# First gate projection of the second block moved into the row gather of the first

## The reference, cut to what matters

```python
h = h + peer(rmsnorm(h, g_ffn[l]), ...)          # gather of chosen rows, dots, weighted sums
h = rmsnorm(h, g_final)
...
proj = x @ w_in_a[a]                             # second block, x is that h
u  = gelu(proj[..., :SG_WIDTH])
gv = gelu(proj[..., SG_WIDTH:2 * SG_WIDTH])
qm = proj[..., 2 * SG_WIDTH:]                    # queries of the memory attention
```

## Time and profile before

| what | us |
|---|---|
| median of three runs | 2060.9 |
| profiled execution, whole | 2064.71 |
| its span, first to last instruction | 2062.8 |
| PE busy in the span | 1768.5 |
| DVE busy | 776.9 |
| gather: first and last issue of L588 | 262.9 to 919.4 |

### The profile page before, as it was taken

How to read it: one execution, slowest core, us unless ns; L and a number is a source line. 1 busy time by engine, 2 the same in 40 slices (tenths; PEclk the granted TensorE clock), 3 DMA queues, 4 the chain that set the end, 5 groups by cost and what they waited for, 6 DMA issues and landing times. The chain is left out here.

```text
span 2062.8 us, 23546 instructions
## 1 busy us (share of the span) xinstructions
PE 1768.5 (86%) x9356; PEld 918.0 (44%) x9356; DVE 776.9 (38%) x1897; ACT 424.3 (21%) x1000; POOL 299.9 (15%) x284
## 2 busy tenths in 40 slices
PE   9999997876655665568999999988899999999887
PEld 7779873552321111124564444333377644433332
DVE  3945178776667777754230000000224300000002
ACT  2481122221221122223111101000223200000001
POOL 0000033543444444430000000000000000000000
PEclk9999998898887667889999999999999999999999
DMA  7237389999999999997789999999964999999997
GB/s 267 93 125 302 143 341 404 397 421 421 420 421 421 421 421 421 421 421 304 315 356 426 426 428 426 428 426 423 420 242 199 378 428 426 427 426 427 426 424 310
DMA packets 81710, 761.82 MB, mean 369 GB/s; under 512 B 9060, under 2 KB 10053, under 8 KB 18102
## 3 DMA queue, kind: packets, MB, share of 16 engines
q1 hardware_dynamic: 43926, 489.35, 56.9%
q0 software_dynamic: 37664, 270.84, 31.9%
HBM read 759.11 MB, written 1.05 MB: 369 GB/s over the span
## 5 line engine op out<-in xcount | busy, mean ns | idle before, releaser
L2683 PE MATMUL bank<-arena 128*64 128x512 f32 x3072 | 680.3, 597 | 42.2 <-DMA arena<-in_w_up 16.8
L1085 PE MATMUL bank<-arena 64*64 64x512 f32 x2032 | 320.4, 784 | 224.4 <-ACT arena L795 224.4
L2683 PEld LDWEIGHTS bank<-arena 128*64 128x64 f32 x3072 | 231.0, 137 | 477.5 <-issue 448.2
L588 POOL DMA_INDIRECT arena<-in_peer_uv,arena x256 | 288.5, 1127 | 614.2 <-PE bank L1085 301.0
L1458 DVE CUSTOM_DVE_ANT_0 arena<-arena 128x1024 f32<-128x1024 f32 x256 | 313.6, 1225 | 156.6 <-DMA arena<-in_peer_uv,arena 153.2
L2811 DVE TENSOR_TENSOR arena<-arena,bank 128x512 f32<-128x512 f32 x32 | 22.0, 687 | 705.7 <-PE bank L2683 705.7
L1085 PEld LDWEIGHTS bank<-arena 64*64 64x64 f32 x2032 | 92.6, 175 | 432.5 <-ACT arena L795 257.0
L844 PE MATMUL bank<-arena 128*128 128x272 f32 (+2 forms) x768 | 144.8, 349 | 0.2 <-ACT arena L614 0.2
L844 PEld LDWEIGHTS bank<-arena 128*128 128x128 f32 x768 | 126.2, 191 | 19.4 <-issue 2.5
L790 ACT ACTIVATE arena<-arena 128x4 f32<-128x4 f32 (+1 forms) x69 | 14.1, 205 | 465.0 <-DVE arena L1458 465.0
L1541 POOL DMA_DIRECT2D arena<-in_w_router x2 | 1.1, 574 | 566.0 <-POOLq L2555 531.3
(11 more groups left out here) (466 smaller groups left out, 1538.0 us busy)
## 6 DMA issues: line engine op xcount, KB each, us to landing
arena<-in_w_gate SPq DMA_DIRECT2D x64, 2048.0 KB, 32.3
arena<-in_w_up SPq DMA_DIRECT2D x56, 2048.0 KB, 32.4
arena<-in_w_down SPq DMA_DIRECT2D x56, 2048.0 KB, 33.2
arena<-in_w_in SPq DMA_DIRECT2D x13, 2048.0 KB, 8.2
arena<-in_w_up SPq DMA_DIRECT2D x16, 1024.0 KB, 38.8
arena<-in_w_down SPq DMA_DIRECT2D x16, 1024.0 KB, 27.0
arena<-in_w_out SPq DMA_DIRECT2D x2, 4096.0 KB, 18.2
arena<-in_wq SPq DMA_DIRECT2D x3, 2048.0 KB, 12.4
```

Of the source, the lines that this page charges most:

```text
L588: nc.gpsimd.indirect_dma_start(SLOT[slot_of[j]], None, d["peer_uv"], bass.IndirectOffsetOnAxis(IDX[:, u % 4, k:k + 1], 0)).then_inc(s_row[ ...
L1085: m = pe.matmul(bank[banks[t][half]][to:to + HALF, :], DIAG[lo:lo + HALF, k + j, :], row[lo:lo + HALF, D + half * 512:D + (half + 1) * 512 ...
L2683: x = pe.matmul(bank[b][j * C:(j + 1) * C, :], operand[:, c, j * C:(j + 1) * C], RING[s % AHEAD][:, c % (DC // 2), j, :], start=(c == 0), ...
```

## The change

SP waits for pick 232 (WIN_A_AFTER) in place of pick 255 before it asks WINA, so the 2 MB load is issued with 23 picks still to land. The products are put in a function first_gate and are issued in two halves of four, the first behind group 61 (picks 244 to 247, after heads' values), the second behind group 62 (picks 248 to 251). Nothing is left behind the last pair.

```diff
+    WIN_A_AFTER = UNITS * R - 6 * Q
     HEADS_FROM = (UNITS - 2) * QUADS
+    A0_AFTER = {HEADS_FROM + 5: range(DC // 2), HEADS_FROM + 6: range(DC // 2, DC)}
...
-            sp.wait_ge(s_row[slot_of[-1]], landed[-1])
+            sp.wait_ge(s_row[slot_of[WIN_A_AFTER]], landed[WIN_A_AFTER])
             sp.dma_start(WINA, ...)
...
+            def first_gate(part):
+                te.wait_ge(s_win_a, 16)
+                for c in part:
+                    m = pe.matmul(bank[A0_BANK][:, :], heads.XT[:, c, :], WINA[:, c, :], start=(c == 0), stop=(c == DC - 1))
+                if c == DC - 1:
+                    m.then_inc(K.s_a0, 1)
...
                         if n == HEADS_FROM + 5:
                             heads.tensor_values(te, pe)
-            te.wait_ge(s_win_a, 16)
-            for c in range(DC):
-                m = pe.matmul(bank[A0_BANK][:, :], heads.XT[:, c, :], WINA[:, c, :], start=(c == 0), stop=(c == DC - 1))
-            m.then_inc(K.s_a0, 1)
+                        if n in A0_AFTER:
+                            first_gate(A0_AFTER[n])
```

## The result

The changed kernel takes 2067.18 us (median of 7 runs, 2065.23 to 2069.96) against 2060.91 us (7 runs, 2057.89 to 2062.00) of the kernel before beside it: ratio 1.0026, interval 1.0015 to 1.0036. By the medians it is 6.3 us slower, by the ratio 5.4 (3.1 to 7.4). The forecast was 2065.8, in the range 2060.9 to 2069.5.

The account below looks back on a forecast made before the run. DMA engines were taken as full in the gather, the first gate behind WINA as ending the stage. Picks 5.2 us late and last pair 2.2 late put b's product 4.9 later: 2060.9 + 4.9 = 2065.8 us, range 2060.9 to 2069.5.

Parts of the forecast that it names:

- Part 1, the load: In the full gather, WINA's 2 MB displace bytes of picks, so picks from about 240 on land 5.2 us later.
- Part 2, the products: On PE at the gather's end, the two halves make the last pair start 2.2 us behind its weights.
- Part 3, what is late next: At the stage's end, barrier 3.3 us later; b's landing and a cold PE make b's product 4.9 us later.
- Part 4, to the end: From the product of b to the run's end, the 4.9 us is carried through unabsorbed, giving 2065.8 us.
- The load is free: Rival for the gather: WINA's bytes flow while picks wait for something else; 2058.2 to 2061.2 us, chance 0.20.
- PE becomes the bound by 5 us or more: Rival for the gather's end: slow or waiting halves push the last pair by 5 us or more; 2068.6 to 2071, chance 0.12.

Follow-up runs that it names:

- e1: The kernel before with one more, unused load of WINA asked at pick 232: median +4.5 us, ratio 1.0026 against the kernel before.
- e4: The changed kernel with 16 filler products behind the last pair to keep PE busy up to the barrier: median +10.5 us, ratio 1.0044 against the kernel before.
- e7: The changed kernel with chunk b asked behind pick 255, so that it lands ahead of the barrier: median +7.1 us, ratio 1.0034 against the kernel before.
- e3: The kernel before with WINA asked at pick 232 and the first gate left at the stage's end: median +5.7 us, ratio 1.0025.
- e6: The kernel before with WINA's load, still behind pick 255, split into two of 1 MB; run twice: medians -1.7 and -2.1 us, ratios 0.9988 and 0.9995.
- e10: The kernel before plus two unused dummy halves of a product at the change's two places: median -0.3 us, ratio 1.0008.
- e2: The changed kernel with WINA's load back behind pick 255 and halves multiplying WIN_Q; run twice: medians +5.6 and +5.0 us against the kernel before, ratios 1.0020 and 1.0016.
- e5: The changed kernel without the eight filler products ahead of the last pair: one run, 2070.55 us.
- e8: The changed kernel with both filler products up to the barrier and chunk b asked behind pick 255: median +2.9 us, ratio 1.0014 against the kernel before.
- e9: e8 without the eight filler products ahead of the last pair: median +4.7 us, ratio 1.0026 against the kernel before.

## Why the prediction was right

**Part 1, the load.** Right, 5.4 us against 5.2, and e1 shows it with PE's program as before. Its picture was wrong: I expected dots 5 us apart twice or so, and went by landings of 10.3 and 13.7 us. It took 28.9 us (e1: 28.8) from issue to landing, with dots some 3.25 us apart (891.70, 894.86, 898.20) where 2.49 is the rule. The price is the bytes all the same. It landed at 912, 22 us before the first half's turn.

**Part 2, the products.** Order and mechanism right, size 1.3 in place of 2.2 us. The sum took group 61 at 5.36 us, and in this execution it ran at 3.66; the 1.2 that I had given as the lower end for that case is what came. The same chain with 5.36, in e4 and e7, made 2.0.

**Part 3, what is late next.** The barrier opened 2.7 us later (959.28 against 954.64, less 1.93), and 3.3 was said: the pair came 0.9 sooner than forecast, the picks 0.2 later, and the barrier opened 0.2 later behind the norm. PE then needed 8.0 us (959.28 to the end of L177 at 967.2) where a warm one needs 5.54: 2.4 us for the lower clock, 2.2 was said. The mis-sized term is b: 8.2 us was taken from the earlier trace rows, and it landed in 10.0. Before, the next loads of the stage were issued 5.4 us behind b (954.59 against 949.21), now 1.4 us behind it (959.23 against 957.82). In the kernels where they follow 3.5 us or more behind, b took 8.0 to 8.4 us (e1, e3, e6 twice, e10), and 9.3 to 10.8 where 1.4 (e2 twice, e4, e5). That these loads take from b is the likely reason; no kernel here moved them alone. So b is later by 6.7 for its issue and 1.8 for its way, less the 2.8 us that it had to spare: 5.7, and the product of b moved by 5.8 (967.91 against 960.18, less 1.93). PE's side gives 5.1. I had taken 4.9, with 5.4 as the upper end, so this step ended beyond its bounds. Two errors partly cancelled, 0.9 us too much for the pair and 1.8 too little for b; that the sum came out as near as 1 us is in part luck.

The Trainium skill's fit of a load (page "DMA: Bandwidth & Descriptors", section "Anatomy of one DMA — SWDGE (gpsimd) path"), for another queue, would have had b land 6.8 us after its issue, an estimate, and PE decide alone. The traces do not agree: 10.0 here, and 8.0 to 8.4 in the kernels where least flowed beside it.

**Part 4, to the end.** 5.9 us at the router, 6.3 in the medians: carried through. The reasoning holds in e1, e4, e6, e7, e8 and e10, whose medians lie within 0.9 us of the stage's shift. In e2, e3 and e9 they are 2 to 5 us above it. In e3 and in e2's repeat the interval still takes the stage's shift in; in e2's first run and in e9 it does not, and there PE's longer stop in the last mixture stands in the trace. So a stage's shift is not always all that an edit does: these two lost time a thousand microseconds behind it, for a reason that stays open.

**The rivals.** "The load is free" fell at its own mark: the last dot was to be less than 1 us later, it is 5.4, and not less in any of the eight profiles with the early load. "PE becomes the bound by 5 us or more" fell too; its milder form, a pair late by 1 to 2 us, is part 2.

## What to carry to other kernels

Before moving a load into a stretch, look whether the DMA engines or the compute engines are full there: in the full gather here 2 MB cost 5.4 us, 5.0 of which are the bytes at the gather's rate, to save a wait of 1.74 us. Work at the end of a stage may be what hides a norm, a barrier and the next load, and what keeps PE at its higher clock, so price what is uncovered before it is moved away. A short wait for one large load may be met better by splitting the load and starting on the first part, if only the first part is needed at first; here that made the stage 1.8 us shorter in two profiles of two.

## What the runs showed of the hardware that I had not expected

- In the full gather a load of 2 MB took 28.7 to 28.9 us from issue to landing, where the same load behind pick 255 took 7.7 in e1; yet the picks lost 5.4 us, not more: it was spread thin, not put behind.
- In e4 PE's lower clock went where the idle time was moved. The same 16 instructions took 7.03 us in e8, and 9.87 behind 3.67 us without work in e4.
- Group 61's 32 instructions took 3.66 us behind 3.47 us of idle time (changed kernel) and 5.36 behind 3.60 (e4), in two kernels whose programs are the same up to there. 1.7 us of difference without any edit is as much as most terms of this study.
- PE stood still in the last mixture for 8.6 to 10.1 us in the three profiles with 9372 matmul instructions on PE, and for 3.6 to 5.5 us in the eleven with 9340, 9356 or 9388, though no instruction there was edited.
